# The first three projections of a block taken in row tiles, each as soon as its eighth of the modulation is known

## The reference

```
mod = c @ w_ada + b_ada                      # c: 1024, w_ada: 1024 x 6144
sh1, sc1, gt1, sh2, sc2, gt2 = split(mod, 6)
h = rms_norm(x, g_pre_mix) * (1 + sc1) + sh1
proj = h @ w_in                              # w_in: 1024 x 5120
bg, cg, u, q, k, v, ga, gb = split(proj)     # 6 of 512 columns, 2 of 1024
y_conv = (bg * conv3(cg * u)) @ w_proj_conv
o = stick_breaking_attention(q, k, v)        # 8 heads of 64
merged = sigmoid(ga) * y_conv + sigmoid(gb) * (o @ w_proj_attn)
x = x + gt1 * rms_norm(merged @ w_out, g_post_mix)
```

## Time and profile before

| | us |
|---|---|
| runs shown: median (lowest, highest) | 844.74 (841.01, 846.2) |
| the profiled execution, its own time | 839.67 |
| its span, first to last instruction | 837.6 |
| first matmul of a product | 37.98 |
| the six products of q, k and v done | 75.31 |

### The profile page before, as it was taken

The page is one execution under the profiler, slowest core; times in us unless marked ns, Lnnn a source line. Parts: engine busy times, 40 slices in busy tenths (PEclk is TensorE's granted clock), DMA queues, the critical chain, the costliest instruction groups (busy, mean ns, idle before and its releaser), DMA issues.

```text
span 837.6 us, 14038 instructions
## 1 busy us (share of the span) xinstructions
PE 788.0 (94%) x6051; PEld 751.4 (90%) x6051; DVE 524.4 (63%) x675; ACT 379.3 (45%) x520; POOL 136.2 (16%) x129
## 2 busy tenths in 40 slices
PE   4599999999979999999998999899799999999997
PEld 3599989999979999999998998596599999999997
DVE  5887667687355776643435899966754665555441
ACT  3443343543433545534334445577654543443441
POOL 1500110001000000000010499804000122221000
PEclk9599999999959999999997989999899999999998
DMA  9979666776414786666541450142514475654511
GB/s 351 361 256 313 190 204 206 240 267 193 157 39 148 255 255 197 203 201 196 163 153 51 153 175 26 56 146 65 186 51 152 151 236 169 200 185 143 189 39 51
DMA packets 123826, 146.00 MB, mean 174 GB/s; under 512 B 3989, under 2 KB 114805, under 8 KB 123765
## 3 DMA queue, kind: packets, MB, share of 16 engines
q1 hardware_dynamic: 122400, 143.32, 52.0%
q10 hardware_dynamic: 1364, 1.79, 0.6%
HBM read 144.05 MB, written 1.05 MB: 173 GB/s over the span
## 4 chain that ended last, share of the span: by engine, by line
PE 81%; DVE 11%; issue 4%; ACT 2%; DMA 1%; POOL 0%; SPq 0%; ACTq 0%; DVEq 0%; POOLq 0%
PE bank L576 69%; DVE mod_acc L1413 2%; DVE w_lo L1421 2%; PE bank L622 2%; DVE score L1775 1%; PE bank L603 1%; DMA raw<-in_w_ada 1%; DVE wide L1714 1%; DVE neg_max L1780 1%; ACT w_hi L1031 1%; PE bank L815 1%; DVE score L1798 1%; PE bank L801 1%; PE bank L611 1%; PE bank L786 1%
## 5 line engine op out<-in xcount | busy, mean ns | idle before, releaser
L1421 DVE TENSOR_TENSOR w_lo<-raw,w_hi 128x2048 fp32r<-128x2048 f32 (+1 forms) x108 | 245.7, 2278 | 144.2 <-ACT w_hi L1031 144.1
L1031 ACT ACTIVATE w_hi<-raw 128x2048 fp32r<-128x2048 f32 (+1 forms) x110 | 206.5, 1881 | 249.6 <-PE bank L576 231.2
L576 PE MATMUL bank<-act_hi,w_hi 128*128 128x256 f32 x816 | 237.5, 291 | 5.5 <-ACT act_hi L1187 2.7
L576 PE MATMUL bank<-act_lo,w_hi 128*128 128x256 f32 x816 | 235.1, 288 | 0.8 <-DVE act_lo L1681 0.4
L576 PE MATMUL bank<-act_hi,w_lo 128*128 128x256 f32 x816 | 234.4, 287 | 0.7 <-DVE w_lo L1421 0.7
L576 PEld LDWEIGHTS bank<-act_hi,w_hi 128*128 128x128 f32 x816 | 160.3, 196 | 9.0 <-issue 8.0
L576 PEld LDWEIGHTS bank<-act_lo,w_hi 128*128 128x128 f32 x816 | 160.2, 196 | 1.9 <-DVE act_lo L1681 0.7
L576 PEld LDWEIGHTS bank<-act_hi,w_lo 128*128 128x128 f32 x816 | 160.3, 196 | 0.9 <-DVE w_lo L1421 0.9
L576 PE MATMUL bank<-hidden_hi,w_hi 128*128 128x256 f32 x432 | 122.5, 284 | 0.8 <-DVE wide L1979 0.8
L576 PE MATMUL bank<-hidden_hi,w_lo 128*128 128x256 f32 x432 | 122.2, 283 | 0.0
L576 PE MATMUL bank<-hidden_lo,w_hi 128*128 128x256 f32 x432 | 122.2, 283 | 0.0
(11 more groups left out here) (268 smaller groups left out, 1043.9 us busy)
## 6 DMA issues: line engine op xcount, KB each, us to landing
raw<-in_w_in SPq DMA_DIRECT2D x31, 1024.0 KB, 5.8
raw<-in_w_ada SPq DMA_DIRECT2D x24, 1024.0 KB, 6.5
raw<-in_w_gate_up SPq DMA_DIRECT2D x22, 1024.0 KB, 5.1
raw<-in_w_mlp_in SPq DMA_DIRECT2D x16, 1024.0 KB, 5.8
raw<-in_w_mlp_out SPq DMA_DIRECT2D x16, 1024.0 KB, 5.2
raw<-in_w_out SPq DMA_DIRECT2D x8, 1024.0 KB, 6.9
raw<-in_w_down SPq DMA_DIRECT2D x8, 1024.0 KB, 5.2
raw<-in_w_down SPq DMA_DIRECT2D x4, 768.0 KB, 4.3
```

Source lines behind the costliest of these rows:

```text
L576: i = e.matmul(dst, lhs, rhs, start=start and k == 0 and m == 0 and n == 0, stop=stop and k == kt - 1 and n == 2, skip_group_check=True)
L1031: e.activation(w_hi[slot][:, 0:kt * n_cols], raw[i % N_RAW][:, 0:kt * n_cols], ACT.Copy).then_inc(hi_split, 1)
L1421: e.tensor_tensor(w_lo[slot][:, 0:kt * n_cols], raw[i % N_RAW][:, 0:kt * n_cols], w_hi[slot][:, 0:kt * n_cols].bitcast(F32), ALU.subtract) ...
```

## The change

- q, k and v no longer are six products one after another. They are eight row tiles of w_in (128 x 1536, 768 KB each). Each tile is used for all six results, which collect in six banks at once (`FIRST_BANKS`). `product_done` counts these eight, so the numbers of all later products move up by two.
- For each row tile k an "ada1" entry loads the columns of shift1 and scale1 that belong to feature tile k: two DMAs of 1024 x 128. VectorE multiplies and adds six of its eight row tiles (128 x 256 each), TensorE takes the other two and the sum over partitions with six matmuls of one column. `scale1`, `shift1`, the activation tile and its low part are made for that k alone. TensorE does k+1's share in the middle of k's matmuls.
- x's rstd comes from ScalarE's squares with a sum along the row, in the layout of the input, and a broadcast by two matmuls; TensorE's eight matmuls of sums of squares and GpSimd's eight products go. The loads of the other row vectors move from ScalarE's queue to SyncE's, their transposes behind c1.
- The six copies from the banks come all together, behind the low parts of c0 and c1. The heads begin before c1 (they began before c0). The products from c on have a ring of four banks.
- The ada chunks of the other four vectors stand behind two of three products from c0 on (before: every second, from q1 on). Other lines only renumber or share semaphores.

```diff
+        DVE_ROWS = 6
...
-        in1_order = [(name, i) for name in ("q", "k", "v", "c", "u", "b", "ga", "gb")
-                     for i in range(in1[name].shape[1] // CHUNK_COLS)]
+
+        FIRST_COLS = 3 * ATTN
+        first_in1 = w("w_in")[:, 3 * CONV:3 * CONV + FIRST_COLS]
+        in1_order = [(name, i) for name in ("c", "u", "b", "ga", "gb") for i in range(in1[name].shape[1] // CHUNK_COLS)]
...
-        ada_order = [(v, r) for v in (SCALE1, SHIFT1, GATE1, SHIFT2, SCALE2, GATE2) for r in range(ADA_CHUNKS)]
-        IN1, PC = 0, 20
...
+        IN1 = DT
+        PC = IN1 + len(in1_order)
...
-            if n % 2 and (n < 6 * ADA_CHUNKS or MLP1 + 2 <= n < MLP1 + 2 + 2 * ADA_CHUNKS):
+            if IN1 <= n < OUT1 and (n - IN1) % 3 != 2 or MLP1 + 2 <= n < MLP1 + 2 + 2 * ADA_CHUNKS and n % 2:
...
-        for _ in range(2 * ADA_CHUNKS):
-            plan_ada()
+        def plan_first_ada(k):
...
+            plan.append(("ada1", k, [w("w_ada")[:, v * D + k * P:v * D + (k + 1) * P] for v in (SHIFT1, SCALE1)]))
...
+        for k in range(DT):
+            plan_first_ada(k)
+            plan_product(first_in1[k * P:(k + 1) * P, :])
         for name, i in in1_order:
             plan_product(in1[name][:, i * CHUNK_COLS:(i + 1) * CHUNK_COLS])
...
+        FIRST_BANKS = {("q", 0): 4, ("q", 1): 5, ("k", 0): 6, ("k", 1): 0, ("v", 0): 1, ("v", 1): 2}
+        MOD1_BANKS = (7, 3)
...
+        banks.ring = [3, 0, 1, 2]
+        banks.pos = len(banks.ring) - 1
...
+        GATE1_AFTER = IN1 + 5
...
+                if kind == "ada1":
+                    for v in range(2):
+                        e.dma_start(raw_view(i)[:, v], source[v].rearrange("(k p) c -> p k c", p=P)).then_inc(
+                            raw_landed[i % N_RAW], 16)
...
+                if i == N_RAW - 1:
+                    for group in (1, 2):
+                        for at, row_source in rows[group]:
+                            e.dma_start(row_tile[group // 2][at:at + row_source.shape[0], :],
+                                        row_source).then_inc(rows_landed[group], 16)
...
-            for i in range(DT // 2):
-                sum_tiles((2 * i, 2 * i + 1), i == 0, i == DT // 2 - 1, (squared, i + 1))
-            modulation_sum(SCALE1)
-            transpose_rows(1)
-            transpose_rows(2)
-            modulation_sum(SHIFT1)
+            b = start_bank("x_rstd")
+            pe.wait_ge(x_rstd, 1)
...
+                             start=tt == 0, stop=tt == TT - 1, skip_group_check=True)
+            t.then_inc(x_spread, 1)
+
+
+            def first_modulation(k):
+
+                b, i = bank[MOD1_BANKS[k % 2]], ada1_at(k)
+                pe.wait_ge(cols_set, 1)
+                if k >= 2:
+                    pe.wait_ge(mod1_set, 2 * (k - 1))
+                pe.wait_ge(*landed(i))
+                src = raw_view(i)
+                for v in range(2):
+                    for r in range(DVE_ROWS, DT):
+                        e.matmul(b[:, v:v + 1], src[:, v, r, :], cols("c", r, 1), start=v == 0 and r == DVE_ROWS, stop=False,
+                                 skip_group_check=True)
+                pe.wait_ge(consts, 1)
+                pe.wait_ge(ada1_scaled, DVE_ROWS * (k + 1))
+                for v in range(2):
+                    t = e.matmul(b[:, v:v + 1], ada1_acc[:, k % 2, v, :], ones[:, 0:1], start=False, stop=True,
+                                 skip_group_check=True)
+                t.then_inc(mod1_summed, 1)
+
+            first_modulation(0)
+            for k in range(DT):
+                slot = k % N_SPLIT
+                for c, (name, i) in enumerate(FIRST_BANKS):
+                    if c == 3 and k < DT - 1:
+                        first_modulation(k + 1)
+                    if k == 0:
+                        start_bank((name, i))
+                    o = bank[FIRST_BANKS[name, i]]
+                    c0 = c * CHUNK_COLS
+                    for m in range(2):
+                        dst = o[:, m * T:(m + 1) * T]
+                        for n, (wp, ap) in enumerate(((w_hi[slot], act_hi), (w_hi[slot], act_lo), (w_lo[slot], act_hi))):
+                            if n == 0:
+                                pe.wait_ge(hi_split, k + 1)
+                                pe.wait_ge(*ready_h1[k][0])
+                            elif n == 1:
+                                pe.wait_ge(*ready_h1[k][1])
+                            else:
+                                pe.wait_ge(*low_ready(k))
+                            if name == "v":
+                                lhs, rhs = ap[:, k, m * P:(m + 1) * P], wp[:, c0:c0 + CHUNK_COLS]
+                            else:
+                                lhs, rhs = wp[:, c0 + m * P:c0 + (m + 1) * P], ap[:, k, :]
+                            t = e.matmul(dst, lhs, rhs, start=k == 0 and m == 0 and n == 0, stop=k == DT - 1 and n == 2,
+                                         skip_group_check=True)
+                t.then_inc(product_done, 1)
 
...
-            for p, (name, i) in enumerate(in1_order):
-                step = p - 6
-                if 0 <= step < HEADS:
-                    stick_scores(step)
+            for step in range(len(in1_order)):
+                p = IN1 + step
                 if 1 <= step <= HEADS:
-                    stick_transpose(step - 1)
-                if 2 <= step < HEADS + 2:
-                    stick_output(step - 2)
-                product(p, start_bank(p), act_hi, act_lo, ready_h1, tokens_first=(name == "v"))
-                if p == 2 * ADA_CHUNKS - 1:
+                    stick_scores(step - 1)
+                if 2 <= step <= HEADS + 1:
+                    stick_transpose(step - 2)
+                if 3 <= step < HEADS + 3:
+                    stick_output(step - 3)
+                product(p, start_bank(p), act_hi, act_lo, ready_h1)
+                if step == 1:
+                    transpose_rows(1)
+                    transpose_rows(2)
+                if p == GATE1_AFTER:
                     modulation_sum(GATE1)
...
-            for group in (1, 2):
-                for at, source in rows[group]:
-                    e.dma_start(row_tile[group // 2][at:at + source.shape[0], :], source).then_inc(rows_landed[group], 16)
+            preload(ACT.Sqrt)
+            act.wait_ge(x_landed, 16)
+            for tt in range(TT):
+                t = e.activation(wide[1][:].rearrange("p k t -> p (k t)")[:, tt * D:(tt + 1) * D], x_nat[:, tt, :], ACT.Square,
+                                 accum_out=x_col[:, 0, tt:tt + 1])
+            t.then_inc(x_squared, 1)
+            act.wait_ge(x_squared, 1)
+            e.activation(x_col[:, 0, :], x_col[:, 0, :], ACT.Sqrt, scale=1.0 / D, bias=eps[:, 0:1]).then_inc(x_rms, 1)
...
-                e.activation(x_T[:, 2 * i:2 * i + 2, :], src, ACT.Copy).then_inc(x_copied, 1)
-                e.activation(squares[:, 2 * i:2 * i + 2, :], src, ACT.Square).then_inc(squared, 1)
-            root(0, D, 1)
-            act.wait_ge(gains_set, 2)
-            act.wait_ge(x_copied, DT // 2)
+                e.activation(x_T[:, 2 * i:2 * i + 2, :], pair(bank[banks.bank["x", i]]), ACT.Copy).then_inc(x_copied, 1)
+            act.wait_ge(x_spread, 1)
+            e.activation(rstd[:], bank[banks.bank["x_rstd"]][:, 0:T], ACT.Copy).then_inc(rstd_set, 1)
             for k in range(DT):
-                e.activation(wide[1][:, k, :], x_T[:, k, :], ACT.Copy, scale=scale1[:, k:k + 1]).then_inc(y_scaled, 1)
...
-            for k in range(DT):
+                high(k)
                 act.wait_ge(y_normed, k + 1)
-                e.activation(act_hi[:, k, :], wide[1][:, k, :], ACT.Identity,
-                             bias=mod[:, SHIFT1 * DT + k:SHIFT1 * DT + k + 1]).then_inc(tiles_hi, 1)
+                act.wait_ge(mod1_set, 2 * k + 2)
...
+                e.activation(act_hi[:, k, :], y, ACT.Identity, scale=scale1[:, k:k + 1],
+                             bias=shift1[:, k:k + 1]).then_inc(tiles_hi, 1)
+                e.activation(y, y, ACT.Identity, scale=scale1[:, k:k + 1], bias=shift1[:, k:k + 1]).then_inc(tile_made, 1)
...
-            stream_to(ADA_CHUNKS - 1)
-            reciprocal(0)
-            stream_to(ADA_CHUNKS + 1)
-            modulation(SCALE1)
...
-            stream_to(2 * ADA_CHUNKS - 1)
-            transpose_rows(1)
-            transpose_rows(2)
-            stream_to(product_at[0])
...
+            e.tensor_scalar(bias1[:], cols("b_ada", SCALE1 * DT, DT), 1.0, None, ALU.add).then_inc(bias1_set, 1)
...
+            def first_rows(k):
+
+                i = ada1_at(k)
+                acc, src = ada1_acc[:, k % 2], raw_view(i)
+                dve.wait_ge(*landed(i))
+                if k >= 2:
+                    dve.wait_ge(mod1_summed, k - 1)
+                for r in range(DVE_ROWS):
+                    if r == 0:
+                        t = e.tensor_scalar(acc, src[:, :, r, :], cols("c", 0, 1), None, ALU.mult)
+                    else:
```

(46 more changed lines are left out.)

224 lines of the change are left out of this document (118 added, 106 removed).

## The result

| | kernel before | changed kernel |
|---|---|---|
| times, median of 13 runs each on one chip (us) | 844.83 | 848.41 |
| lowest, highest | 840.76, 849.94 | 847.06, 853.34 |
| profiled execution, span | 837.6 | 845.3 |

The ratio is 1.0054, with a 95% interval of 1.003 to 1.0078: the change made the kernel 0.5% slower, which is within the 1% called no change and above the noise. The forecast was 841 us, with 833 to 851 as its range.

The account below looks back on a forecast made before the run. Bound by TensorE's work wherever fed, so time comes from the unfed start. Terms -7.2 + 1.0 + 1.9 + 0.4 = -3.9 from 839.67 gave 835.8; carried over to the runs' median, 841 us, range 833 to 851.

Parts of the forecast that it names:

- q, k and v end: End of the eight row tiles: forecast at 68.1 us, 7.2 us earlier than 75.31.
- first scores, first transposes: TensorE's waits for VectorE's backlog behind q, k and v: +1.0 us at the scores, +1.9 us at the transposes.
- transposes of the rows: Transposes of the row vectors, formerly in idle time, now stand behind c1: +0.4 us.
- First matmul and pace: Start of the tiles: first product matmul at 17.5 us, 20.5 earlier; then 6.0 us per tile.
- Half of tile 0 at 1.2 GHz: First tile: half its matmuls at the lower clock, taking 3.7 us, so tile 1 begins at 27.2.
- The tiles' rivals: In the eight tiles: clock falls again (14%, 857 to 873 us), or short 512 B packets bound them (6%, 854 us).
- Three ada chunks: Chunks, 7.8 us of VectorE, moved from under q, k and v to later products: 0, up to +7.8 without cover.
- The backlog grows: Rival, 14%: the moved ada chunks meet no cover, +4 to +8 us, 845 to 849, no change.
- my stalls there: Forecast waits of TensorE behind q, k and v: 1.0 us at the first scores, 1.9 at the first transposes.
- The weights' 1.0 us: GpSimd's weights of the first head, taken as 1.0 us and ending at 85.2, with TensorE wanting them at 83.2.
- The waits after 110 us should be those of before: Sign to check: TensorE's waits past 110 us stay as in the kernel before.
- The rule that I had weighed against the change: Skill page: frequent short idles between matmul groups make the clock swing; by it 857 us would be the forecast.

Follow-up runs that it names:

- experiment 1: Changed kernel with no ada chunk behind c0, c1 and u0, the twelve chunks standing later and GATE1's sum two products later; 0.9993 of the kernel before, median 843.4 us.
- experiment 4: Kernel before with only the ada chunks placed as in the change, GATE1's sum four products later; 0.9996 of the kernel before.
- sixth experiment: Changed kernel with one ada chunk moved from behind u1 to behind b1, nothing else; 1.0061 of the kernel before.
- twelfth profile: Changed kernel with early mixed_hi, ada chunks moved off c0, c1 and u0, GATE1's sum two products later; 0.9933 of the kernel before, median 835.0 us.
- 5: Changed kernel with ScalarE's first mixed_hi ahead of w_hi and the gate of its product; 1.0003 of the kernel before, median 843.85 us.
- experiment 7: Kernel before with the eight heads beginning one product later on all engines, nothing else; 0.9995 of the kernel before.

## Why the prediction was wrong

It named the gain at the start rightly and lost it behind it. By its own terms, in us:

| step | forecast | measured |
|---|---|---|
| q, k and v end | -7.2 | -9.3 (66.0 against 75.31) |
| first scores, first transposes | +1.0, +1.9 | +0.8, +3.9 |
| transposes of the rows | +0.4 | +0.5 |
| clock behind the first transposes | 0 | +1.9 (product 1.5, transposes 0.4) |
| clock behind GATE1's sum | 0 | +1.5 (0.8 of it in the product of 6.70) |
| last weight_T, and the clock behind it | 0 | +1.9, +1.5 |
| merge (C-D) | 0 | -1.0 |
| norm and start of the MLP (D-E) | 0 | +1.9 |
| sum | -3.9 | +3.6; E came 4.4 later |

- **First matmul and pace: right.** 16.65 for 17.5 (the six one-column matmuls took 1.5 us, where I had taken 2.6 at 1.2 GHz), and 6.03 us per tile for 6.0. The clock fell and came back (0.50 in 15 to 21 us), some 3 us earlier than taken; the two make the 2.1 us by which q, k and v ended early. (Half of tile 0 at 1.2 GHz is 18 x 0.22 = 4.0 us, where my sum had 3.7.) The tiles' rivals did not come: the clock stayed at 1.00 from 22 to 66 us, one-column matmuls and all, and the 512 B packets kept up, with little to spare: 311 GB/s at a mean DMA share of 0.97, from 20 to 62 us ScalarE waited 7.1 us in all for loads, VectorE and TensorE not at all.
- **The step that failed: "Three ada chunks ... I cost them at 0; if that cover is gone, up to +7.8."** I looked for their cover at 150 to 160 us and did not place them one by one where the heads begin. There, behind c0, c1 and u1, they met the copies, two low parts at once and a queue that the tiles had left with one product in stock (c0's `w_hi` waits for no load, c1's 1.14 us, u0's 4.42). Taking the two behind c0 and c1 away gave 6.8 us back in A-B (experiment 1); my stalls there came to 2.9. The same chunks at the same products cost nothing in the kernel before (experiment 4): the price is that of what they meet there. So the rival "The backlog grows", which I gave 14%, is what came, and the measured 848.4 lies within its 845 to 849; its +4 to +8 had neither the clock nor weight_T in it.
- **The weights' 1.0 us** came from the earlier trace rows, a row with VectorE idle beside it. My weights ended at 85.2, and so they did (85.06), but because two errors met: the scan was 2 us earlier and GpSimd 1.9 us slower. TensorE was there at 81.2 instead of 83.2, so the time from 81.2 on was all wait. GpSimd ended 0.5 us, half of its own 1.0, after VectorE's second multiply-add (84.56); the sixth experiment shows 1.00 without them. The Trainium skill, "SBUF — State Buffer", section "Who interferes with whom", has the rule: the pair of ports that VectorE and GpSimd share is an exclusive lock, and an instruction of VectorE with two inputs in SBUF contends with one of GpSimd that reads SBUF. These runs agree: the multiply-adds kept their 2.61 us, and GpSimd waited for them. It is not a price by itself, though: in the first and twelfth profile GpSimd took 2.34 us beside a TENSOR_SCALAR and one multiply-add, and TensorE did not wait for it.
- **"The waits after 110 us should be those of before" was wrong.** The chain went through weight_T at 154 (experiments 4, 5 and 7). I checked the order of instructions around c1, not at the end of the heads, where weight_T slid behind VectorE's idle 4.35 us.
- **The clock was taken as a risk of the tiles only.** It fell at three places that waits or a sum had opened, for 4.9 us together. Of these the 1.5 behind GATE1's sum cannot be put down to the change: it fell there in two of the three profiles of the kernel before and its variants as well (experiments 4 and 7), only not in the one that I compare with. It fell behind the wait at the first transposes (3.6 to 4.4 us) in every profile that had it unfilled; behind the 1.9 us and behind the sum in some and not in others. The rule that I had weighed against the change, short idles that come often (the Trainium skill, "TensorE: Matmul & The Clock Gate", section "A second HAM failure mode: psum-queue depth-cycling"), would have had the clock swing in the tiles. These runs do not bear it out: TensorE was busy 5.88 of every 6 us there, and the clock stayed at 1.00. What harm the clock did lay behind the tiles.
- D-E is the same code and ran from 68.9 to 73.8 us in the profiles, so its +1.9 is no effect that I can give to the change. C-D came 1.0 shorter with the chunks' new places: the kernel before with these places has 33.02 (experiment 4), with its own and later heads 34.13 (experiment 7). The 0.8 us between the sum and E stay without a name.
